# Forgetting attention of two mixers: heads scored in couples on distinct rows of TensorE

## What is computed

```
def forgetting_attention(q, k, v, f_logit):
    scale = 1.0 / float(np.sqrt(dh))
    c = jnp.cumsum(jax.nn.log_sigmoid(f_logit.astype(jnp.float32)), axis=1)
    for blk in range(s // Q_BLOCK):
        qs, qe = blk * Q_BLOCK, (blk + 1) * Q_BLOCK
        sc = jnp.einsum('bhqd,bhkd->bhqk', qh[:, :, qs:qe], kh[:, :, :qe]).astype(jnp.float32) * scale
        sc = sc + (c[:, :, qs:qe, None] - c[:, :, None, :qe])
        sc = jnp.where(causal[None, None], sc, -jnp.inf)
        pr = jax.nn.softmax(sc, axis=-1).astype(vh.dtype)
        outs.append(jnp.einsum('bhqk,bhkd->bhqd', pr, vh[:, :, :qe]))
```

## Time and profile before

| | us |
|---|---|
| median of 3 runs | 3266.39 |
| lowest and highest | 3265.86, 3267.04 |
| the profiled execution, own time | 3267.23 |
| its span | 3265.4 |
| attention, second block's layer 0 (first scores to first PS<-AS matmul) | 1430.06 to 1558.94 |
| the same, layer 1 | 2568.34 to 2695.97 |

### The profile page before, as it was taken

How to read it: one execution, slowest core, us unless ns; L and a number is a source line. 1 busy time by engine, 2 the same in 40 slices (tenths; PEclk the granted TensorE clock), 3 DMA queues, 4 the chain that set the end, 5 groups by cost and what they waited for, 6 DMA issues and landing times.

```text
span 3265.4 us, 42751 instructions
## 1 busy us (share of the span) xinstructions
PE 3132.7 (96%) x17872; PEld 2498.3 (77%) x17872; DVE 1778.8 (54%) x2424; ACT 1120.7 (34%) x1586; POOL 63.3 (2%) x65
## 2 busy tenths in 40 slices
PE   7788888899999999999999999999999999999997
PEld 4666865788888888776788888888887767888886
DVE  4535665534355434687764344753446877643446
ACT  3322245333243222335443223532233354422233
POOL 0002310000000000000000000000000000000000
PEclk8898999999999999999999999999999999999999
DMA  6231000232222322221222323323222212223222
GB/s 247 96 116 60 29 2 31 79 97 97 97 97 97 97 97 91 91 80 46 85 94 100 97 97 91 108 96 100 97 85 94 77 52 84 97 98 97 97 87 74
DMA packets 81935, 290.09 MB, mean 89 GB/s; under 512 B 9552, under 2 KB 11216, under 8 KB 81232
## 3 DMA queue, kind: packets, MB, share of 16 engines
q1 hardware_dynamic: 81744, 287.36, 26.2%
HBM read 285.23 MB, written 2.10 MB: 88 GB/s over the span
## 4 chain that ended last, share of the span: by engine, by line
PE 91%; DVE 5%; issue 2%; ACT 2%; DMA 1%; POOL 0%; SPq 0%; DVEq 0%; ACTq 0%; POOLq 0%
PE PS L1396 79%; PE PS L1478 3%; PE PS L1720 1%; PE PS L1683 1%; PE PS L1722 1%; PE PS L1411 1%; DVE XD L2174 1%; PE PS L1741 1%; PE PS L1730 1%; PE PS L1607 0%; PE PS L1671 0%; DVE SM L2361 0%; ACT SPL L1771 0%; PE PS L1702 0%; PE PS L1431 0%
## 5 line engine op out<-in xcount | busy, mean ns | idle before, releaser
L1396 PE MATMUL PS<-HS,SPL 128*128 128x512 f32 (+1 forms) x7752 | 1804.5, 393 | 9.2 <-DVE HS L2106 7.3
L1396 PEld LDWEIGHTS PS<-HS,SPL 128*128 128x128 f32 (+1 forms) x7752 | 1455.5, 189 | 330.4 <-issue 21.1
L2058 DVE TENSOR_TENSOR SPL<-RAW,SPL 128x1024 fp32r<-128x1024 f32 (+1 forms) x491 | 584.0, 1193 | 722.7 <-ACT SPL L1771 718.9
L1771 ACT ACTIVATE SPL<-RAW 128x1024 fp32r<-128x1024 f32 (+1 forms) x491 | 503.0, 1028 | 843.7 <-PE PS L1396 843.5
L1396 PE MATMUL PS<-FF,SPL 128*128 128x512 f32 x2880 | 654.6, 389 | 0.0
L1396 PEld LDWEIGHTS PS<-FF,SPL 128*128 128x128 f32 x2880 | 540.7, 188 | 112.1
L2450 DVE SCALAR_TENSOR_TENSOR CA<-AP__146,CW,CA 128x512 f32<-128x512 f32 x240 | 180.0, 750 | 6.2
L1959 ACT ACTIVATE FF<-TMP 128x512 fp32r<-128x512 f32 x88 | 55.7, 633 | 234.8 <-DVE TMP L2420 234.8
L1953 ACT ACTIVATE SA<-SA 128x512 f32<-128x512 f32 x88 | 55.5, 633 | 191.7 <-DVE SA L2410 191.7
L2410 DVE TENSOR_TENSOR SA<-PS,R 128x512 f32<-128x512 f32 x88 | 60.5, 691 | 98.8 <-PE PS L1396 98.5
L2422 DVE TENSOR_TENSOR FF<-TMP,FF 128x512 fp32r<-128x512 f32 x88 | 60.9, 692 | 66.1 <-ACT FF L1959 66.1
(11 more groups left out here) (294 smaller groups left out, 2238.5 us busy)
## 6 DMA issues: line engine op xcount, KB each, us to landing
RAW<-in_w_ff_in SPq DMA_DIRECT2D x176, 512.0 KB, 3.6
RAW<-in_w_in SPq DMA_DIRECT2D x88, 512.0 KB, 3.7
RAW<-in_w_ff_out SPq DMA_DIRECT2D x80, 512.0 KB, 3.5
RAW<-in_w_ff SPq DMA_DIRECT2D x64, 512.0 KB, 3.6
MW<-in_w_mod SPq DMA_DIRECT2D x48, 512.0 KB, 4.6
RAW<-in_w_out SPq DMA_DIRECT2D x24, 512.0 KB, 3.7
RAW<-in_w_ple_gate SPq DMA_DIRECT2D x16, 512.0 KB, 3.6
XT<-in_xT SPq DMA_DIRECT2D x2, 2048.0 KB, 7.7
```

What stands on the lines that cost most here:

```text
L1396: m = pe.matmul(o, w[x][:, k, rows], r.T[:, r.k0 + k, y, 0:r.cols], start=r.start and k == 0 and (x, y) == (0, 0), stop=r.stop and k == r. ...
L1771: a.activation(SPL[:, s, 0, 0:n], RAW[:, s, 0:n], AF.Copy).then_inc(w_hi, 1)
L2058: v.tensor_tensor(SPL[:, s, 1, 0:n], RAW[:, s, 0:n], SPL[:, s, 0, 0:n], ALU.subtract).then_inc(w_lo, 1)
```

## The change

Heads are taken in couples (0 and 1, 2 and 3, ...). A step w of 16 scores the same query block of both heads together: q times k of both (rows 0 to 63 and 64 to 127), then the forget term of both (rows 0 to 31 and 32 to 63), then both masks, into banks 0 and 1. For this the forget rows (CF, FH, CL, RH, SEL2) lie on 64 partitions instead of 32, the small weight `w_f_2` is 64 columns wide instead of 32, and `f_row` runs once per couple, four times instead of eight. `attention` now turns both units of step w-2, yields, scores step w, yields.

```
-        dense(W["w_f_2"][l], 8, HS, None, ev_f, 32)
+        dense(W["w_f_2"][l], 8, HS, None, ev_f, 64)
...
+        def f_scores(w):
+            t = Rec()
+            t.p, t.qb = w // 4, w % 4
+            if t.qb == 1 and t.p < 3:
+                f_row(t.p + 1)
+            t.uses = (take(0), take(1))
+            t.waits = [qk_ready["q", t.p], qk_ready["k", t.p], rh_ready[t.p]] if t.qb == 0 else []
+            emit("f_scores", t)
+            if t.qb == 3:
+                rh_after[t.p % 2] = t.uses[1].mark
+            for hh in range(2):
+                s = Rec()
+                s.u = 2 * w + hh
+                s.h, s.qb = 2 * t.p + hh, t.qb
+                s.pb_after = pb_after[s.u % 5]
+                softmax_rows(s, (t.uses[hh],), 128 * (s.qb + 1), PB2[s.u % 5], SM2[:, :, s.u % 6])
...
         def attention():
-            whole, m = None, None
-            for u in range(37):
+            whole = None
+            for w in range(19):
                 if whole:
                     f_values(*whole)
-                if 4 <= u < 36:
-                    m = f_turn(u - 4)
-                if u < 32:
-                    f_scores(u)
+                if 2 <= w < 18:
+                    f_turn(2 * w - 4)
+                    m = f_turn(2 * w - 3)
+                    yield 1
+                if w < 16:
+                    f_scores(w)
                 else:
                     scale_rows()
-                whole = (units[u - 4][0] - 1, m) if 4 <= u < 36 and (u - 4) % 8 == 7 else None
-                if u % 3:
-                    yield 1
+                whole = (2 * ((w - 2) // 4), m) if 2 <= w < 18 and w % 4 == 1 else None
+                yield 1
...
+            for hh, u in enumerate(t.uses):
+                r = slice(64 * hh, 64 * hh + 64)
+                pe.matmul(PS[:, u.b, 0:n], QK[r, t.p, 0, cols], QK[r, t.p, 1, 0:n], start=True, stop=False)
+            for hh, u in enumerate(t.uses):
+                r = slice(32 * hh, 32 * hh + 32)
+                pe.matmul(PS[:, u.b, 0:n], CL[r, cols], RH[r, t.p % 2, 0:n], start=False, stop=False)
+            for u in t.uses:
+                pe.matmul(PS[:, u.b, n - 128:n], idb[:, :], causal[:, :], start=False, stop=True).then_inc(full[u.b], 1)
```

More of the change, by code:

```diff
@@ L1136, in build, with f_row @@
         as_ready = [None] * 4
-        def f_row(h):
+        def f_row(p):
             t = Rec()
-            t.h, t.L, t.after, t.done = h, L, rh_after[h % 2], count(s_rh)
+            t.p, t.L, t.after, t.done = p, L, rh_after[p % 2], count(s_rh)
             emit("f_row", t)
[L1142 to L1156, removed]
+            rh_ready[p] = t.done
+        def f_scores(w):
[14 more added lines that the diff above has]
+                softmax_rows(s, (t.uses[hh],), 128 * (s.qb + 1), PB2[s.u % 5], SM2[:, :, s.u % 6])
         def f_turn(u):
@@ L1160, in f_turn @@
             s.u = u
-            s.h, s.qb = units[u]
+            s.h, s.qb = 2 * (u // 8) + u % 2, u % 8 // 2
             s.use, s.p, s.after = take(2 + u % 2), p_ready[u], pt_after[s.h % 2]
@@ L1712, in v_turned, with f_scores @@
             m.then_inc(full[r.u2.b], 1)
[L1714 to L1717, removed]
+        def f_scores(t):
+            n = 128 * (t.qb + 1)
+            cols = slice(128 * t.qb, n)
+            for w in t.waits:
                 pe.wait_ge(*w)
[L1719 to L1723, removed]
+            for u in t.uses:
+                opened(u)
+            for hh, u in enumerate(t.uses):
[4 more added lines that the diff above has]
+                pe.matmul(PS[:, u.b, 0:n], CL[r, cols], RH[r, t.p % 2, 0:n], start=False, stop=False)
+            for u in t.uses:
+                pe.matmul(PS[:, u.b, n - 128:n], idb[:, :], causal[:, :], start=False, stop=True).then_inc(full[u.b], 1)
         def f_turn(s):
@@ L1966, in f_logit @@
         def f_logit(r):
-            t = TMP[0:32, r.slot, :]
+            t = TMP[0:64, r.slot, :]
             if r.after:
@@ L2457, in f_logit @@
         def f_logit(r):
-            t = TMP[0:32, r.slot, :]
+            t = TMP[0:64, r.slot, :]
             v.wait_ge(*r.L.last)
             v.wait_ge(*r.use.mark)
-            v.tensor_tensor(CF[:, :], PS[0:32, r.use.b, :], R[0:32, :], ALU.mult).then_inc(free[r.use.b], 1)
+            v.tensor_tensor(CF[:, :], PS[0:64, r.use.b, :], R[0:64, :], ALU.mult).then_inc(free[r.use.b], 1)
             v.wait_ge(*r.use.rel)
-            v.tensor_scalar(CF[:, :], CF[:, :], vec(f"bf_{r.L.l}")[0:32, :], None, ALU.add).then_inc(s_fl, 1)
+            v.tensor_scalar(CF[:, :], CF[:, :], vec(f"bf_{r.L.l}")[0:64, :], None, ALU.add).then_inc(s_fl, 1)
             v.wait_ge(*r.act)
@@ L2472, in f_logit @@
             v.wait_ge(*r.high)
-            v.tensor_scalar(t, FH[:, :], SEL2[:, 19:20], None, ALU.mult).then_inc(v_own, 1)
+            v.tensor_scalar(t, FH[:, :], SEL2[:, 11:12], None, ALU.mult).then_inc(v_own, 1)
             own.n += 1
             v.wait_ge(v_own, own.n)
-            v.scalar_tensor_tensor(out=CF[:, :], in0=CF[:, :], scalar=SEL2[:, 18:19], in1=t, op0=ALU.mult,
+            v.scalar_tensor_tensor(out=CF[:, :], in0=CF[:, :], scalar=SEL2[:, 10:11], in1=t, op0=ALU.mult,
                                    op1=ALU.add).then_inc(v_own, 1)
@@ L2683, in constants @@
     c["c_dftd"] = np.concatenate([np.where(same, np.cos(pd), 0), np.where(same, np.sin(pd), 0)], 1).astype(f) / f(8.0)
[L2684 to L2693, removed]
+    sel = np.zeros((64, 12), f)
+    for o in (0, 32):
+        sel[o:o + 16, 0] = 1
+        sel[o + 16:o + 32, 1] = 1
+        for p in range(4):
+            for n in (0, 8):
+                sel[o + 16 + n + 2 * p + o // 32, 2 + p] = -1
+                sel[o + n + 2 * p + o // 32, 6 + p] = 1
+    low = (np.arange(64) // 8) % 2
+    sel[:, 10] = low
+    sel[:, 11] = 1 - 2 * low
     c["c_sel"] = sel
@@ L2732 @@
     A["w_in_2"] = np.stack([pieces(np.concatenate([wi[l][:, :1536], wi[l][:, 1544:]], 1)) for l in range(2)])
-    A["w_f_2"] = np.stack([rows(np.concatenate([wi[l][:, 1536:1544]] * 4, 1)) for l in range(2)])
+    A["w_f_2"] = np.stack([rows(np.concatenate([wi[l][:, 1536:1544]] * 8, 1)) for l in range(2)])
     A["p"] = np.stack([rows(x["p_2"][l, 0].T) for l in range(2)])
```

14 lines of the change are left out of this document (7 added, 7 removed).

## The result

The changed kernel takes 3278.48 us (median of 5 runs, 3276.33 to 3281.16) against 3266.32 for the kernel before on the same chip (5 runs, 3263.73 to 3267.04): a ratio of 1.0037, 95% interval 1.0026 to 1.0048. That is 12.2 us slower, where 7.1 were forecast, and inside the range of 3261 to 3289. The profiled execution has a span of 3275.8 us and a mean granted clock of 0.976.

The account below looks back on a forecast made before the run. PE's dense products (79% of the chain) were taken as the bound. An attention takes 97.1 + 36.8 = 133.9 us: layer 0 +5.0, layer 1 +6.3, the wait at L1438 -4.2, together +7.1, giving 3273.5 us, range 3261 to 3289.

Parts of the forecast that it names:

- covered part: Attention from first scores to those of step 12, scored among dense blocks: 97.1 us, including the waits for bank 3.
- A pair: Scores of two heads together take one head's time plus small extras: 1.75 us at 512 keys, 5.3 a couple.
- the wait for bank 3: Turn right after a group of values waits for ACT and DVE: 2.0 us first, 1.2 second, bounds 0 and 2.3.
- DVE keeps up, just: In the covered part DVE needs 32.8 us for a couple's four steps, PE 33.3, with one block (2.85 us) of slack.
- DVE falls behind: Rival: half-clock stretch at the first values, end of 38.2 us, +5 in each layer over forecast, 3284 us; chance 0.25.
- signs of being wrong: End under 33 us, PE waiting among covered blocks beyond the two turns, or a pair costing what two units cost.
- The bare end: Attention from step 12's scores on, without blocks: DVE's queue sets the pace, mostly half clock, 36.8 us.
- What comes back: Behind the output projection DVE is early with the convolution, so the 2.11 us wait at L1438 goes in each layer.
- At nothing: Forget rows on 64 partitions, four `f_row` less and the 64-column `w_f_2` cost nothing; without cover, half a microsecond.
- the clock holds and the waits hide: Rival: end at 2.4 GHz, bank 3 at half cost, attention 128.5 us, -3.7 us in all, 3262.7; chance 0.22.
- Row tiles do not overlap: Rival: each covered couple costs 3.7 us more, the end 1, 12 in each layer, 3298 us; chance 0.08.

Follow-up runs that it names:

- e5: The changed kernel with two convolution taps per tick instead of three from the attention on, the rest behind the attention: 3257.01 us, 0.9976.
- e3: The changed kernel with the convolution's 18 taps of the attention's block-free last part recorded behind it, beside the output projection: 3278.7 us, 1.0031.
- e9: The kernel before with only the forget rows on 64 partitions and the 64-column small weight, scores still head by head: 3264.59 us, 0.9995.
- e1: The changed kernel with the two heads of a step issued one after the other: a single execution of 3297.25 us.
- e10: e6 with the matmul of the convolution's sum of squares recorded four blocks behind the sums instead of two: 3238.24 us, 0.9907.
- e4: The changed kernel with 24 yields instead of 35, spreading the whole attention over the 24 blocks: 3258.83 us, 0.9968.
- e6: The changed kernel with 24 yields and, in steps with values, the yield between values and turns: 3245.63 us, 0.9941.
- e7: e6 with two taps per tick in the attention and the convolution's sum of squares recorded behind the second gate's first product: 3249.12 us, 0.995.

## Why the prediction was right, step by step

**The direction and the mechanism held.** PE's saving was real and was paid away by waits. The size was 5.1 us short, and the terms that make it up err in both directions, so that the sum is nearer than its terms deserve. With the pairs at their measured cost the same sum would have given 3.6 us less (1.8 in each covered part), +3.5 instead of +7.1, against +12.2:

- *A pair.* Forecast 1.75 us at 512 keys and 5.3 for a couple; measured 1.58 and 4.7 (0.77, 1.04, 1.31 and 1.58 by size). I charged 0.05 for each second product and 0.1 for the second mask; together they cost 0.03 at 512 keys and 0.06 at the smaller sizes. With four couples this favours the kernel by 2.4 us a layer. The Trainium skill ("TensorE: Matmul & The Clock Gate", Part 3) puts a further tile at about 4 ns; q times k for a pair took 1.06 us, as for one head, so the trace agrees as far as it resolves.
- *Covered part.* Forecast 97.1, measured 100.70. Without the surplus on the pairs (three couples, 1.8 us) it would have been forecast at 95.3, so the miss is 5.4 us. The failing step is the wait for bank 3. I gave 2.0 and 1.2 us; they were 1.39 and 5.23. Behind the second comes a block of 5.00 us for 3.01, where I had kept the clock at 1.00. Bank 3 is +3.4, the block +2.0, a wait of 0.84 us for DVE's scaling (at 1486.24) comes on top: 6.2, so the rest of the covered part must have been some 0.8 cheaper than I summed it.
- *Why it failed* is the sentence "DVE keeps up, just". I summed DVE's own work to 32.8 us against PE's 33.3 and left out its waits. The own work was right. From the low part of the first values to that of the second DVE is busy 32.37 us, but takes 38.89:

```profile
1469.27:1508.16 38.89, 32.70 (x164) 22.93 (x164) 32.37 (x59) 19.54 (x37) 0.00 (x0) 0.98 0.18 54
```

  Of the 6.5 us between, 1.64 and 1.65 are the waits for ACT shown above, 2.38 a wait for PE's scores at 1474.51, and the rest are short gaps. With a margin of 0.5 us for a couple, the 3.3 us for ACT alone are enough to make DVE late. They could have been read in the trace of before, whose attention has as many such waits. Before, then after (waits in total, times, longest):

```profile
DVE SPL L2058 <- ACT SPL L1771: 5.9, 4, 2.5
DVE SPL L2067 <- ACT SPL L1780: 5.9, 4, 2.4
```

  e5 shows it from the other side: with fewer taps the wait is 1.25 us and the covered part 92.90. I had bounded this wait at 2.3 us, the wait of before, which is no upper bound for a queue that lags. The mishap was in the rivals, as "DVE falls behind", but I put its cost at the first values and at the end; it came at the second values. One of my signs of being wrong, a wait of PE among the covered blocks beyond the two turns, showed too, in small: the 0.84 us, and 0.17 at 1493.83.
- *The bare end.* Forecast 36.8, measured 35.78. The layout was close: third values at 8.1, measured 8.4; last scaling at 28.9 to 30.7, measured 29.4; half clock for most of it, measured 6.8 and 17.1 us. That the end "is DVE's queue" was right only in part. Without its 15 us of taps, e3 still takes 31.00. The chain between engines, ACT's gate and the half clock hold the rest. How much of it is half clock alone no run separates.
- *What comes back.* Forecast -2.1 a layer, measured -2.3. e3 confirms the reason: with the taps moved out of the end, the wait returned as 1.80 us.
- *At nothing.* The 64 forget rows: e9 gives 0.9995.

In sum: covered part +3.6, end -1.0, so an attention +2.6 in layer 0 (136.48 against 133.9) and +2.4 in layer 1, together +5.0, the projections -0.4. Of the 5.1 us between forecast and medians 0.5 stay open. The term that was mis-sized is the second wait for bank 3 with its slow block.

The rivals: "the clock holds and the waits hide" did not happen here, but it is what e5 did in its covered part. "Row tiles do not overlap" fell with e1.

## What to carry to other kernels

When one engine's steps become cheaper, the work interleaved with them has to be dealt out again. Here a saving of 17 us a layer on PE (four couples at 4.3) was a loss of 8 in the attention with 35 yields on 24 blocks, and became a gain of 15 (e10) when the 24 blocks carried all the steps and one block stood between a group of values and the turn that needs its bank. For an engine that "just keeps up", count its waits for the other engines too, and take no wait of before as an upper bound. Follow the work that leaves a stretch: in e3, e4, e6 and e7, taps taken out of the attention came back as a wait of 2 to 8 us at the next matmul that needs them. e10, which let that matmul stand two blocks later, has little of it left. e7, which moved it behind a whole product with fewer taps done before, had the longest wait of all.

## What the runs showed of the hardware

- A second row tile of q times k (64 rows, 512 columns, fp32) costs no time that the trace resolves: 1.06 us for two heads as for one. The forget term on 32 rows likewise: 0.43 us for two, as for one in e1. A serial issue of the same instructions takes 3.16 us instead of 1.58.
- The granted clock fell to 0.50 within the wait of 5.23 us (window 1506.60 to 1513.40), and the block after it took 5.00 us for 3.01: a wait costs more than its length. In the end it fell at 1533.90, 0.3 us before the wait of 3.63 us began. Since the last block PE had then done only scores and a turn, with one wait of 1.28 us. It fell again at 1547.50, where PE had done little but transposes and one pair of scores between waits of 1.29, 1.10 and 0.82 us:

```profile
1543.17 0.30 PE L1739 MATMUL PS<-ident,PB 128*128 128x128 f32 x1 [1.29 <-DVE AS L2514]
...
1546.24 0.44 PE L1739 MATMUL PS<-ident,PB 128*128 128x128 f32 x2 [1.10 <-DVE PB L2377]
1547.50 2.08 PE L1727 MATMUL PS<-QK 64*128 64x512 f32 x4 [0.82 <-ACT PB L1913]
```

  Two waits of 1.26 and 1.25 us in e5, with dense blocks behind them, left it at 1.00, and the blocks there kept their 3.0 us.
